# Expert rows scaled by their gates on leaving PSUM, and summed into nine row buffers by adding gathers

## The reference

```python
x = layer_norm(ALPHA * h + mix @ w_out)                 # first half of a layer
pg = softmax(x @ w_gr + b_gr)                           # expert group
gate = g_p * top_p / sum(top_p)                         # two experts of 8 in that group, two gates a token
yb[block] = (silu(xe @ w_g[e]) * (xe @ w_u[e])) @ w_d[e]  # rows of a block of one expert e
y = segment_sum(yb * buf_w[:, None], buf_t)             # each token: gate0 * row0 + gate1 * row1
h = layer_norm(ALPHA * x + y)                           # LN with eps 1e-5, ALPHA = sqrt(2)
p = h @ w_in                                            # the next layer's projection
```

## Time and profile before

| | |
|---|---|
| times of 3 runs | 3747.36, 3750.14, 3765.46 us; median 3750.14 |
| the profiled execution: its time, its span | 3730.53, 3728.5 us |
| mean granted PE clock in it | 0.907 |
| busy share of the span | PE 87%, DVE 34%, ACT 24%, POOL 16% |
| DMA | 519 MB moved, mean 139 GB/s |

### The profile page before, as it was taken

The page is one execution under the profiler, slowest core; times in us unless marked ns, Lnnn a source line. Parts: engine busy times, 40 slices in busy tenths (PEclk is TensorE's granted clock), DMA queues, the critical chain, the costliest instruction groups (busy, mean ns, idle before and its releaser), DMA issues.

```text
span 3728.5 us, 54744 instructions
## 1 busy us (share of the span) xinstructions
PE 3242.1 (87%) x22252; PEld 2008.2 (54%) x22252; DVE 1274.4 (34%) x3192; ACT 912.9 (24%) x1913; POOL 584.4 (16%) x587
## 2 busy tenths in 40 slices
PE   7997888998889979999499878899898999699990
PEld 3445667777666544333244566777767755334330
DVE  4103444444443351111341134444434434411116
ACT  0001233434442101111110113334434321011111
POOL 1000011111100013343300001111111000243333
PEclk9995899999999989999699869899989899799995
DMA  6112122222213229994721211222221132599826
GB/s 251 53 39 64 44 76 76 76 76 73 73 54 114 86 81 404 408 416 174 280 88 39 83 33 62 76 76 76 76 71 51 50 125 78 215 386 414 349 80 225
DMA packets 168757, 519.40 MB, mean 139 GB/s; under 512 B 41472, under 2 KB 82368, under 8 KB 143168
## 3 DMA queue, kind: packets, MB, share of 16 engines
q0 software_dynamic: 65600, 337.74, 23.6%
q1 hardware_dynamic: 83328, 106.86, 9.2%
q10 hardware_dynamic: 19584, 71.31, 4.9%
HBM read 630.21 MB, written 86.89 MB: 192 GB/s over the span
## 4 chain that ended last, share of the span: by engine, by line
PE 75%; DVE 9%; DMA 7%; ACT 4%; issue 2%; DVEq 2%; POOL 0%; ACTq 0%; SPq 0%; POOLq 0%
PE ps L770 65%; PE ps L767 10%; DMA w_slots<-in_w_gu,rowA 4%; DVE grams L2126 2%; DMA c_x<-xd 1%; DVE S_all L2524 1%; ACT PT L1863 1%; DVE PT L2547 1%; DVE c_x L2162 1%; DMA c_b<-ybd,dga 0%; ACT S_all L1832 0%; ACT kT L1591 0%; ACT PT L1591 0%; DMA xb<-xd,idall 0%; DVE t L2126 0%
## 5 line engine op out<-in xcount | busy, mean ns | idle before, releaser
L770 PE MATMUL ps<-w_slots,xbT 128*64 128x512 f32 (+1 forms) x2048 | 468.4, 609 | 27.3 <-DMA w_slots<-in_w_gu,rowA 23.4
L770 PE MATMUL ps<-hT,w_in 128*128 128x512 f32 x896 | 390.6, 597 | 3.2 <-ACT hT L1591 3.2
L770 PEld LDWEIGHTS ps<-w_slots,xbT 128*64 128x64 f32 x2048 | 175.0, 140 | 276.7 <-issue 261.8
L770 PE MATMUL ps<-grams 128*128 128x128 f32 (+1 forms) x2448 | 294.2, 276 | 29.5 <-DVE grams L2126 23.1
L770 PEld LDWEIGHTS ps<-grams 128*128 128x128 f32 (+1 forms) x2448 | 272.1, 188 | 51.0 <-issue 28.0
L770 PEld LDWEIGHTS ps<-hT,w_in 128*128 128x128 f32 x896 | 170.9, 192 | 216.1 <-issue 211.0
L770 PE MATMUL ps<-w_out,o_mixT 128*128 128x512 f32 x576 | 260.9, 600 | 1.3 <-DVE o_h L2745 1.3
L1591 ACT ACTIVATE kT<-ps 128x512 f32<-128x512 f32 x320 | 188.1, 596 | 254.4 <-PE ps L767 252.4
L770 PE MATMUL ps<-w_slots,hidT 128*64 128x512 f32 (+1 forms) x1024 | 233.9, 598 | 1.2 <-ACT hidT L1591 1.2
L2914 DVE SCALAR_TENSOR_TENSOR gt<-gt,ps 128x256 f32<-128x256 f32 x64 | 26.9, 421 | 517.8 <-ACT gt L2071 517.8
L767 PE MATMUL ps<-cst,S_all 128*128 128x128 f32 x832 | 159.9, 311 | 20.3 <-ACT PT L1591 20.3
(11 more groups left out here) (376 smaller groups left out, 5139.8 us busy)
## 6 DMA issues: line engine op xcount, KB each, us to landing
ybd<-yb ACTq DMA_DIRECT2D x64, 512.0 KB, 8.3
pd<-stage SPq DMA_DIRECT2D x56, 256.0 KB, 2.5
out_y<-c_h ACTq DMA_DIRECT2D x27, 512.0 KB, 2.9
w_in<-in_w_in SPq DMA_DIRECT2D x6, 2048.0 KB, 25.4
o_mixT<-mixd SPq DMA_DIRECT2D x18, 512.0 KB, 3.5
o_h<-out_y SPq DMA_DIRECT2D x18, 512.0 KB, 4.7
xd<-o_x ACTq DMA_DIRECT2D x18, 512.0 KB, 2.8
c_x<-xd ACTq DMA_DIRECT2D x18, 512.0 KB, 6.8
```

The costliest lines, as they stand in the source:

```text
L770: return pe.matmul(out, lhsT, rhs, start=start, stop=stop, skip_group_check=True)
```

## The change

The copies out of PSUM multiply each row by its gate, divided by ALPHA. For this, routing also makes a table `gslot` (row by pair) of the gates: one more DVE product with the one-hot table, 18 more small PE products after those for `idall`, one more PE product behind the first pair's transposes, and two small DVE copies. As the layer norm doesn't change when its whole input is scaled, `x + y / ALPHA` takes the place of `ALPHA * x + y`, with eps divided by ALPHA squared, and ACT's scaling pass is gone. The sum is made by the gathers: `add_first` adds the token's first expert row onto the residual in `c_x`, `add_second` the second one, once the first has landed; DVE's two multiply-adds are gone. `c_x` has nine buffers, one for each tile, in the room of `c_a`, `c_b` and the old `c_x`; all nine residual tiles are loaded right behind the last expert store, and each tile has its own semaphores. At `l = 0` four tiles are loaded ahead in place of three. SP's `w_in` load no longer waits for gathers.

Before, the second row and the last two were not there. The core of the diff:

```diff
@@ sync: load_w_in
-                if l:
-                    sp.wait_ge(ya_in[2], 32 * (3 * (l - 1) + 1))
@@ gpsimd
-            def gather(l, t):
-                if t >= 3:
-                    pool.wait_ge(dve_m.sem, dve_m.at(("norm", l, t - 3), "v"))
-                for k, c in enumerate((c_a, c_b)):
-                    pool.indirect_dma_start(c[t % 3][:], None, ybd[:], bass.IndirectOffsetOnAxis(ap=dga[:, TILES * k + t:TILES * k + t + 1], axis=0)).then_inc(ya_in[t % 3], 16)
+            def add_first(l, t):
+                pool.wait_ge(x_in[t], 16 * (l + 1))
+                pool.indirect_dma_start(c_x[t][:], None, ybd[:], bass.IndirectOffsetOnAxis(ap=dga[:, t:t + 1], axis=0),
+                                        compute_op=ALU.add).then_inc(ya_in[t], 16)
+            def add_second(l, t):
+                pool.wait_ge(ya_in[t], 16 * l)
+                pool.indirect_dma_start(c_x[t][:], None, ybd[:], bass.IndirectOffsetOnAxis(ap=dga[:, TILES + t:TILES + t + 1], axis=0),
+                                        compute_op=ALU.add).then_inc(yb_in[t], 16)
...
-                for t in three:
-                    gather(l + 1, t)
-                for t in range(TILES):
+                for t in range(5):
+                    add_first(l + 1, t)
+                for t in four:
+                    add_second(l + 1, t)
+                add_first(l + 1, 5)
+                ln_root(("norm", l + 1, 0))
...
+                for t in range(3, TILES):
                     ln_root(("norm", l + 1, t))
                     if t + 3 < TILES:
-                        gather(l + 1, t + 3)
+                        add_second(l + 1, t + 3)
@@ tensor
+                pe.wait_ge(dve_m.sem, dve_m.at(("route", l), "goh"))
+                for c in range(2 * TILES):
+                    g = 32 * (c % 4)
+                    m = mm(Q[2][g:g + 32, P:2 * P], r_gown[:, c, :], r_col[:, c, :], c < 4, c >= 2 * TILES - 4)
+                m.then_inc(pe_m.sem, pe_m.mark(("route", l), "gpart"))
...
                 xT(0)
+                pe.wait_ge(dve_m.sem, dve_m.at(("route", l), "gpart"))
+                mm(Q[3][:, 64:64 + NPAIR], r_gpart, cst[:, C_SEL4:C_SEL4 + 32], True, True).then_inc(pe_m.sem, pe_m.mark(("route", l), "gsel"))
@@ scalar
-                act.dma_start(c_x[t % 3][:], src[t * P:t * P + P]).then_inc(x_in[t % 3], 16)
-            def scaled(l, t):
-                act.wait_ge(x_in[t % 3], 16 * (l * 3 + t // 3 + 1))
-                act.activation(c_x[t % 3][:], c_x[t % 3][:], ACT.Copy, scale=ALPHA).then_inc(act_m.sem, act_m.mark(("norm", l, t), "ax"))
+                act.dma_start(c_x[t][:], src[t * P:t * P + P]).then_inc(x_in[t], 16)
...
-                if t + 3 < TILES:
-                    load_x(l, t + 3)
+                if l == 0 and t + 4 < TILES:
+                    load_x(l, t + 4)
...
-                    cp(yb[:, 512:1024], pD[:, 512:1024]).then_inc(act_m.sem, act_m.mark(k, f"dn{p}"))
+                    act.activation(yb[:, 512:1024], pD[:, 512:1024], ACT.Copy, scale=gslot[:, p:p + 1]).then_inc(act_m.sem, act_m.mark(k, f"dn{p}"))
...
-                for t in three:
+                for t in range(TILES):
                     load_x(l + 1, t)
@@ vector
-                    dve.wait_ge(ya_in[u], 32 * (3 * (l - 1) + t // 3 + 1))
-                    dve.wait_ge(act_m.sem, act_m.at(("norm", l, t), "ax"))
-                    for k, c in enumerate((c_a, c_b)):
-                        dve.scalar_tensor_tensor(c_x[u][:], c[u][:], gates[:, k, t:t + 1], c_x[u][:], ALU.mult, ALU.add)
-                        dve.drain()
-                variance(("norm", l, t), c_x[u])
+                    dve.wait_ge(yb_in[t], 16 * l)
+                    variance(("norm", l, t), c_x[t], 1e-5 / ALPHA ** 2)
...
-                tt(gates[:, 0, :], s2, cst[:, C_VALID:C_VALID + TILES], ALU.mult)
+                dve.scalar_tensor_tensor(gates[:, 0, :], s2, 1 / ALPHA, cst[:, C_VALID:C_VALID + TILES], ALU.mult, ALU.mult)
...
+                tt(r_gown, r_own[:], bc(gates[:].rearrange("p k t -> p (k t)"), [P, 2 * TILES, NPAIR]), ALU.mult).then_inc(dve_m.sem, dve_m.mark(k_, "goh"))
...
-                    dve.tensor_copy(yb[:, 0:512], pD[:, 0:512]).then_inc(dve_m.sem, dve_m.mark(k, f"yb{p}"))
+                    dve.tensor_scalar(yb[:, 0:512], pD[:, 0:512], gslot[:, p:p + 1], None, ALU.mult).then_inc(dve_m.sem, dve_m.mark(k, f"yb{p}"))
```

More of the change, by code:

```diff
@@ L195, in plan @@
                 if t < TILES:
-                    T["act"].plan(("norm", l, t), ["ax"])
                     T["dve"].plan(("norm", l, t), ["v"])
@@ L205, in plan @@
                 T["act"].plan(("proj", l), [s])
-            elif l:
-                T["act"].plan(("norm", l, int(s[1])), ["ax"])
         for s in DVE_PROJ:
@@ L253, in plan @@
         T["pe"].plan(("lg", l, NPT), ["xT", "lg"])
-        T["pe"].plan(("route", l), ["rank", "be", "part", "ids"])
+        T["pe"].plan(("route", l), ["rank", "be", "part", "ids", "gpart"])
         T["act"].plan(("route", l), ["e1", "e2"])
-        T["dve"].plan(("route", l), ["E7", "E8", "diag", "rows", "oh0", "oh1", "part", "ids"])
-        T["pe"].plan(("moe", l), ["xT0", "gu0", "xT1"])
+        T["dve"].plan(("route", l), ["E7", "E8", "diag", "rows", "oh0", "oh1", "goh", "part", "ids", "gpart", "gslot"])
+        T["pe"].plan(("moe", l), ["xT0"])
+        T["pe"].plan(("route", l), ["gsel"])
+        T["pe"].plan(("moe", l), ["gu0", "xT1"])
         T["act"].plan(("moe", l), ["xT0", "gu0", "xT1"])
@@ L281, in build @@
         consts_in, zero_out = sem("consts_in"), sem("zero_out")
-        x_in, y_out, ya_in = ([sem(f"{n}{u}") for u in three] for n in ("x_in", "y_out", "ya_in"))
+        y_out = [sem(f"y_out{u}") for u in three]
+        x_in, ya_in, yb_in = ([sem(f"{n}{t}") for t in range(TILES)] for n in ("x_in", "ya_in", "yb_in"))
         lnr_in, state_in, w_mix_in, window_in = (sem(n) for n in ("lnr_in", "state_in", "w_mix_in", "window_in"))
@@ L307, in build @@
         dga = sb("dga", [P, 2 * TILES], I32)
-        idall = sb("idall", [P, NPAIR], I32)
+        idall, gslot = sb("idall", [P, NPAIR], I32), sb("gslot", [P, NPAIR])
         rowA, rowB, offA = sb("rowA", [P, NPAIR], I32), sb("rowB", [P, NPAIR], I32), sb("offA", [1, NPAIR], I32)
@@ L313, in build @@
         with ExitStack() as s:
-            c_a, c_b, c_x, c_h = ([sb(f"c_{n}{u}", [P, D], scope=s) for u in three] for n in "abxh")
+            c_x, c_h = ([sb(f"c_{n}{u}", [P, D], scope=s) for u in range(k)] for n, k in (("x", TILES), ("h", 3)))
             lnr = sb("lnr", [P, 2 * D], scope=s)
@@ L1649, in project @@
             def project(l):
-                def ax(t):
-                    if l:
-                        scaled(l, t)
-                ax(0)
-                ax(1)
-                ax(2)
                 for t in three:
@@ L1658, in project @@
                     transposed_rows(l, t)
-                    ax(t + 3)
                 store_rows(l, 3)
@@ L2114, in _ @@
                 experts(l)
-            for t in three:
-                scaled(L, t)
             for t in range(TILES):
                 store_rows(L, t)
-                if t + 3 < TILES:
-                    scaled(L, t + 3)
         @block.vector
@@ L2126, in tt, with variance @@
                 return dve.tensor_tensor(out, x, y, op)
-            def variance(stage, x):
+            def variance(stage, x, eps=1e-5):
                 u = stage[2] % 2
@@ L2134, in variance @@
                 dve.drain()
-                dve.tensor_scalar(lnt[:, u, 2:3], lnt[:, u, 1:2], 1e-5, None, ALU.add).then_inc(dve_m.sem, dve_m.mark(stage, "v"))
+                dve.tensor_scalar(lnt[:, u, 2:3], lnt[:, u, 1:2], eps, None, ALU.add).then_inc(dve_m.sem, dve_m.mark(stage, "v"))
             def normalized(stage, x, out, g):
@@ L2151, in norm_x @@
                     dve.wait_ge(pe_m.sem, pe_m.at(("proj", l), f"h{t - 3}"))
[L2152 removed]
+                normalized(("norm", l, t), c_x[t], c_h[u], lnr)
             def norm_v(l, t):
[L2155 removed]
                 if l == 0:
[L2157 to L2164 removed]
+                    dve.wait_ge(x_in[t], 16)
+                    variance(("norm", 0, t), c_x[t], 1e-5)
+                else:
+                    dve.wait_ge(yb_in[t], 16 * l)
+                    variance(("norm", l, t), c_x[t], 1e-5 / ALPHA ** 2)
             def norm(l, t):
@@ L2907, in route @@
                 dve.tensor_copy(idall[:], Q[3][:, 0:NPAIR]).then_inc(dve_m.sem, dve_m.mark(k_, "ids"))
+                dve.wait_ge(pe_m.sem, pe_m.at(k_, "gpart"))
+                dve.tensor_copy(r_gpart, Q[2][:, P:2 * P]).then_inc(dve_m.sem, dve_m.mark(k_, "gpart"))
+                dve.wait_ge(pe_m.sem, pe_m.at(k_, "gsel"))
+                dve.tensor_copy(gslot[:], Q[3][:, 64:64 + NPAIR]).then_inc(dve_m.sem, dve_m.mark(k_, "gslot"))
+                dve.drain()
             def experts(l):
```

24 lines of the change are left out of this document (15 added, 9 removed).

## The result

The changed kernel takes 3758.2 us (median; 3744.4 to 3768.9), the kernel before 3749.5 us (3734.4 to 3765.5) on the same chips. The ratio is 1.0023, 95% interval 1.0013 to 1.0033: slower, by 8.7 us where 11.6 us of gain were forecast. The time lies inside the forecast range, its sign does not. The profiled execution took 3755.9 us with a span of 3754.1; that of before was a quick one for its kernel (granted clock 0.907 against 0.900), so of the 25.6 us between the two spans only what lies in the four places of the prediction is read as the change. The rest lies in the main in the two stretches from a layer's first feature product to its routing, which the change leaves alone: they are 12.2 and 6.2 us longer, with 21.8 us more of PE's busy time for the same 18,400 instructions.

What follows compares the result with a forecast made beforehand. The prediction saw PE's chain as the bound, with gains only where PE waits for DVE: layer gap and end. Terms -4.2 + 1.1 - 15.5 + 4 - 3 + 6 = -11.6 us gave 3738.5 us, range 3720 to 3768.

Steps and rivals of the forecast that it cites:

- Start: First layer: with four loads ahead DVE no longer waits for tile 3's load, so PE's first feature product comes 4.2 us sooner.
- Routing: Routing: DVE's extra product delays the `r_part` copy and so PE's first transposes, 0.57 us a layer, +1.1 us in all.
- DVE's tile: Layer gap and end: without the two multiply-adds, a tile's turn on DVE falls from 7.1 to 4.43 us.
- Start of tile 0: Waiting for the adding gathers, DVE gets tile 0 11 us later at the end and 15 us later between the layers.
- End and layer gap at factor 1: If adds cost the same as plain gathers, the end gains 15.5 us and the gap between the layers 3 us.
- The price of an add: An add takes 1.5 times a plain gather's engine time, costing +4 us at the end and +6 between the layers.
- rival C: An add takes the engines twice as long or more, making both gaps DMA-bound; +5 us at 2, +23 at 2.5; 22%.
- 9 us of slack: At the end the DMA engines have 47 us of work and 56 us to do it before tile 8's add is wanted.
- Rival B: In both gaps an add costs no more than a plain gather: -21.6 us in all, 3728.5 us; chance 31%.
- Rival D: Late loads hold up POOL's queue, so DVE waits 1.5 us more on each tile: 3749 us, no change; chance 7%.
- landmark A: Signs of the main forecast (40%): between layers, first feature product at PE's end + 57 us; at the end, last norm near + 69.
- only moves the crowd: Between the layers the engines are full anyway, so issuing `w_in` 15 us earlier only shifts the crowding; no size of its own.

Runs made afterwards that it cites:

- e1_plain: The changed kernel with both adding gathers made plain, so the sum is left out: ratio 0.989 to the kernel before, layer gap 54.4 us, end 69.6 us.
- e6_pool_busy: e1_plain with a small POOL instruction ahead of each gather, imitating an add's longer issue: layer gap 55.3 us, end 70.9 us, one run.
- e4b_order_late: The changed kernel with adds issued in order of need and `w_in` held until tile 2's rows landed: layer gap 64.5 us, end 85.3 us, one run.

## Why the prediction was wrong

- **Start, -4.2:** right, -4.4 in the profile (31.32 against 35.69), and -4.2 when done alone. DVE no longer waits at tile 3.
- **Routing, +1.1:** the copy of `r_part` came 0.49 us later to PE (idle 0.88 instead of 0.39). At the first routing `xb` still landed 9.6 us after PE's first product there, as before; at the second 0.5 us later. So +0.5, too small to tell.
- **DVE's tile, 7.1 to 4.43:** right, 4.30 from one statistics to the next.
- **Start of tile 0, 11 and 15 us later at factor 1:** right. With plain gathers in the same queue (e1_plain) it is 12 us (25.9 against 14.0) and 16 us (30.2 against 14.1). Between the layers two errors nearly cancel, which is luck: in e1_plain the fifth load was there 16.8 us after PE's end, not 19, and tile 0's second gather took 12.2 us from its issue to DVE's start, not 8.7.
- **End and layer gap at factor 1, -15.5 and -3:** right, e1_plain has -16.9 and -3.3.
- **The price of an add, factor 1.5, +4 and +6: this step failed.** The factor is 1.94, and the price came to +15.1 at the end and +18.9 between the layers: 34 us instead of 10. Two things are in that. The factor itself: I chose between bytes touched (three streams against two) and bytes read, and it is the count of reads that comes near 1.94; 1.19 us more for each add instead of 0.64. (That the reads are the cause is the Trainium skill's reason in the section named above; the runs show the price alone.) And the cover: the formula of rival C at 1.94 gives 12.4 us between the layers and 18 x 1.19 - 9 = 12.4 us at the end, 25 us of the 34. I had taken a fifth of it as hidden in the layer gap, where nothing was: 13 x 1.19 is 15.5, all of it real. At the end the 9 us of slack covered only 21.4 - 15.1 = 6.3: no slack lies ahead of tile 0, where DVE's start alone moved by 8.7 us (34.6 against 25.9), and my landmark for it, PE's end + 25, had no price of an add in it. That leaves about 3 us in each gap against the formula's terms. Some 1 us of it may be POOL's issue (e6_pool_busy, one run); the rest I can't place.
- **Rival C** named the mechanism, the place and the factor, and its landmarks were met (last norm 81 us after PE's end, layer gap over 65, a DMA share over 1 at far below 413 GB/s). Its sum at 1.93, +3 us, was 5.7 us short, and it had 22% where the 1.93 of the Trainium skill spoke for more. I had weighed byte counts of my own more heavily than a measured ratio for an add in the DMA engines; the read count was in the text as an alternative and is the one whose number was met.
- **Rival B** falls: an add costs 1.19 us more. A part was covered at the end, where 21.4 us more of engine time cost 15.1; none between the layers. **Rival D** (waits on each tile) shows only on single tiles: the fifth (4.83 us), the sixth (1.53 us) and the second (0.74 us) at the end, the fifth (10.38 us) and the second (1.45 us) between the layers.
- **Slips in the forecast's own numbers:** landmark A for the layer gap, + 57, doesn't follow from its sum (57.7 - 3 + 6 = 60.7), nor + 69 for the last norm (about 71 with the 4 us). And by its own formula C at a factor of 2 to 2.3 is +5 to +16 us, inside the 19 us called no change, so "slower by more: most of C" gave too much to that class.
- **`w_in` "only moves the crowd":** nearly right. Alone its delay gives 1.0 us, which is within the scatter; it is worth 6 us only where tile 2's rows come sooner (e4b_order_late).

## What to carry to other kernels

Before a vector add is moved into an adding DMA, ask whether the DMA engines are full in that stretch: here each such add took 1.19 us more of all 16 engines to save 1.28 us of one engine, and it paid for one of a tile's two rows, not for both. Price an adding transfer at nearly twice a plain one (1.94 here), and count everything that is queued ahead of the first tile, since no slack behind it helps the first consumer. Splitting the change showed that its side parts were good by themselves: the fourth load at the start, and the gates applied at the copy that was made anyway (0.9969 without a single add).

## What the runs showed of the hardware

- An adding gather of 512 KB into SBUF: 213 and 210 GB/s at a full DMA share, 2.46 us of the 16 engines; a plain one 413 GB/s, 1.27 us. By the queue's packet time at the end the difference is 1.21 us.
- Its issue on POOL takes 1.53 to 1.57 us against 0.93 to 0.98 for a plain one; next to large DVE instructions it took 1.6 to 2.6 us, a plain one up to 1.95.
- From issue to landing an add took 14.8 us in the median among other transfers, a plain gather in the same queue and place (e1_plain) 9.0, in the kernel before 8.2 and 8.7.
- The copies out of PSUM with a scale from a column are not quite as short as plain ones: 0.69 us instead of 0.60 on ACT and 0.75 instead of 0.69 on DVE for 128x512.
